# A transformer in one kernel: weight tiles woven column by column in SBUF, and the two TensorE operands placed 128 bytes apart

## The reference, cut to what matters

```
def swiglu(x, w_gate, w_up, w_down):
    return (jax.nn.silu(x @ w_gate) * (x @ w_up)) @ w_down
...
        x = x + 0.5 * rmsnorm(swiglu(h, w1_gate[i], w1_up[i], w1_down[i]), g_ffn1_post[i])
        h = rmsnorm(x, g_mix_pre[i])
        (sb_q, sb_k, sb_v, c_q, c_kv, k_rope_raw, cv_b, cv_c, cv_h) = jnp.split(h @ w_in[i], split_at, axis=-1)
...
        x = x + rmsnorm(mixed @ w_out[i], g_mix_post[i])
```

## Time and profile before

| | before |
|---|---|
| three runs | 3332.34, 3334.76, 3337.73 us; median 3334.76 |
| span of the profiled execution | 3337.3 us |
| matmuls, PE busy | 19480, 3229.6 us (97%) |
| weight loads, PEld busy | 2729.8 us (82%) |
| DVE, ACT, POOL busy | 2059.6, 1359.2, 1345.4 us |
| DMA | 362.59 MB, mean 109 GB/s |

### The profile page before, as it was taken

How to read it: one execution, slowest core, us unless ns; L and a number is a source line. 1 busy time by engine, 2 the same in 40 slices (tenths; PEclk the granted TensorE clock), 3 DMA queues, 4 the chain that set the end, 5 groups by cost and what they waited for, 6 DMA issues and landing times.

```text
span 3337.3 us, 51827 instructions
## 1 busy us (share of the span) xinstructions
PE 3229.6 (97%) x19480; PEld 2729.8 (82%) x19487; DVE 2059.6 (62%) x2673; ACT 1359.2 (41%) x2335; POOL 1345.4 (40%) x643
## 2 busy tenths in 40 slices
PE   8999999999999999999999999998999999999998
PEld 7998775789877899877579987765789987879986
DVE  7774444586647876354477765678477734477753
ACT  5553225344435445322444543324435521254542
POOL 6320562554116541065164404656553107635300
PEclk9999999999999999999999999999999999999999
DMA  4543221255332454322035533221145433215532
GB/s 156 159 143 104 90 87 32 70 152 151 114 123 83 138 160 120 105 83 87 19 99 153 153 117 108 101 68 34 51 135 166 123 103 108 82 57 146 168 104 95
DMA packets 99977, 362.59 MB, mean 109 GB/s; under 512 B 11088, under 2 KB 11344, under 8 KB 99536
## 3 DMA queue, kind: packets, MB, share of 16 engines
q1 hardware_dynamic: 88704, 320.90, 29.4%
q0 software_dynamic: 7776, 28.32, 5.1%
q10 hardware_dynamic: 3312, 10.86, 0.9%
HBM read 355.84 MB, written 4.19 MB: 108 GB/s over the span
## 4 chain that ended last, share of the span: by engine, by line
PE 73%; DVE 10%; issue 6%; ACT 4%; POOL 3%; DMA 3%; DVEq 0%; ACTq 0%; POOLq 0%; SPq 0%
PE psC L749 4%; PE psC L751 4%; PE psC L750 4%; PE psA L749 4%; PE psA L751 4%; PE psA L750 4%; PE psD L899 2%; PE psD L900 2%; PE psD L901 2%; PE psB L899 2%; PE psB L900 2%; PE psB L901 2%; DVE WL L2240 2%; DMA Y<-in_ws 2%; PE psB L984 2%
## 5 line engine op out<-in xcount | busy, mean ns | idle before, releaser
L629 POOL TENSOR_TENSOR WH<-raw,scalars 128x1024 fp32r<-128x1024 f32 (+1 forms) x194 | 377.8, 1948 | 1206.5 <-DMA raw<-in_w 1143.3
L2240 DVE TENSOR_TENSOR WL<-raw,WH 128x1024 fp32r<-128x1024 f32 x324 | 447.9, 1385 | 70.5 <-POOL raw L663 39.8
L631 POOL TENSOR_TENSOR WL<-raw,WH 128x1024 fp32r<-128x1024 f32 (+1 forms) x194 | 471.2, 2429 | 15.2
L1697 ACT ACTIVATE WH<-raw 128x1024 fp32r<-128x1024 f32 x324 | 340.4, 1053 | 48.9 <-DMA raw<-in_ws 37.2
L2316 DVE TENSOR_TENSOR WL<-raw,WH 128x1024 fp32r<-128x1024 f32 (+1 forms) x144 | 163.1, 1135 | 307.4 <-ACT WH L1718 305.8
L658 POOL TENSOR_TENSOR raw<-raw,Y 128x1024 f32<-128x1024 f32 x54 | 133.4, 2471 | 509.6 <-DMA raw<-in_ws 509.6
L1718 ACT ACTIVATE WH<-raw 128x1024 fp32r<-128x1024 f32 (+1 forms) x144 | 141.9, 989 | 375.7 <-DMA raw<-in_w 375.7
L749 PE MATMUL psA<-HH,WH 128*128 128x512 f32 x560 | 230.0, 411 | 0.0
L751 PE MATMUL psA<-HL,WH 128*128 128x512 f32 x560 | 218.5, 390 | 0.0
L750 PE MATMUL psA<-HH,WL 128*128 128x512 f32 x560 | 218.3, 390 | 0.0
L899 PE MATMUL psD<-TH,WH 128*128 128x256 f32 x720 | 202.0, 281 | 6.2 <-DVE psC L2287 2.7
(11 more groups left out here) (540 smaller groups left out, 9631.1 us busy)
## 6 DMA issues: line engine op xcount, KB each, us to landing
raw<-in_w SPq DMA_DIRECT2D x338, 512.0 KB, 3.5
raw<-in_ws SPq DMA_DIRECT2D x216, 512.0 KB, 3.6
Y<-in_ws SPq DMA_DIRECT2D x54, 512.0 KB, 4.7
raw<-in_ws POOLq DMA_DIRECT2D x54, 512.0 KB, 5.4
X<-in_x ACTq DMA_DIRECT2D x4, 512.0 KB, 9.5
NRAW<-in_mem ACTq DMA_DIRECT2D x2, 1024.0 KB, 7.2
out<-Y SPq DMA_DIRECT2D x8, 256.0 KB, 2.1
POSI<-in_pos ACTq DMA_DIRECT2D x4, 256.0 KB, 2.6
```

The source lines that it names most:

```text
L629: pool.tensor_tensor(WH[j][:, 0:w], raw[j][:, 0:w], zero[:, 0:1].broadcast_to([P, w]), ALU.subtract).then_inc(w_hi, 1)
L631: pool.tensor_tensor(WL[j][:, 0:w], raw[j][:, 0:w], WH[j][:, 0:w], ALU.subtract).then_inc(w_split, 1)
L1697: act.activation(WH[slots[i]][:], DX if i == 6 else raw[slots[i]][:], ACT.Copy).then_inc(part_hi, 1)
L2240: dve.tensor_tensor(WL[slots[i]][:], DX if i == 6 else raw[slots[i]][:], WH[slots[i]][:], ALU.subtract).then_inc(part_lo, 1)
```

## The change

The host interleaves each two neighbouring tiles column by column: column c of tile 2j is float 2c of their 256, and column c of tile 2j+1 is float 2c+1. The kernel reads a tile as 128 floats with a step of two (`woven`). Buffers are shifted, so that every weight slot begins at byte 0 modulo 256 and every activation tensor that is a moving operand of the products with pieces begins at byte 128. Some small tensors are laid over others to make room. The pieces of the latent heads, of five tiles at most, are now split six tiles wide, since tile 4 shares its columns with tile 5.

```
-    slot_at = [region(8 * KB) for _ in range(RING)]
+    region(LINE)                     # LINE = 128
+    slot_at = [region(8 * KB) for _ in range(RING)]
...
+    region((LINE - at[0]) % (2 * LINE))
     ar = region(88 * KB)
-    slot_at += [ar + 72 * KB, ar + 80 * KB, ar + 28 * KB, ar + 36 * KB, ar + 64 * KB, SQo, Yo + 8 * KB]
+    slot_at += [ar + 72 * KB - LINE, ar + 80 * KB - LINE, ar + 28 * KB - LINE, ar + 36 * KB - LINE, ar + 64 * KB - LINE, SQo, Yo + 8 * KB]
...
-    sum_at = [ar + 48 * KB, ar + 56 * KB, ar + 72 * KB, ar + 80 * KB]
+    sum_at = [ar + 48 * KB - 2 * LINE, ar + 56 * KB - 2 * LINE, ar + 72 * KB, ar + 80 * KB]
...
+    woven = lambda t: slice(t // 2 * 2 * P + t % 2, (t // 2 + 1) * 2 * P, 2)
...
-            rounds(MH, KQ + KKV)
+            rounds(MH, KQ + KKV + 1)
...
-                w = slice((first_tile + t) * P + cols[0], (first_tile + t) * P + cols[1])
+                w = woven(first_tile + t)
                 pe.matmul(out, WH[slot][:, w], hi[:, t], start=start and t == 0, stop=False)
                 pe.matmul(out, WL[slot][:, w], hi[:, t], start=False, stop=False)
...
-                    w = slice((half * HALF_K + k) * P, (half * HALF_K + k + 1) * P)
+                    w = woven(half * HALF_K + k)
...
+    weave = lambda w: np.ascontiguousarray(w.reshape(-1, P, TILES // 2, 2, P).swapaxes(3, 4)).reshape(-1, P, TILES * P)
+    return weave(out), weave(pairs)
```

More of the change, by code:

```diff
@@ L147, in sb @@
         return nc.alloc_sbuf_tensor_at(name, list(shape), dt, offset=o)
-    KB = 1024
+    KB, LINE = 1024, 128
     X = sb("X", [P, KD, S])
@@ L171, in program @@
     VALL = sb("VALL", [P, DEPTH * NV + NW])
-    VL = sb("VL", [P, NV])
+    VLo = region(320)
+    VL = sb("VL", [P, NV + 4], offset=VLo)
     tabM = sb("tabM", [P, 2, S])
-    scalars = sb("scalars", [P, 4])
+    scalars = VL[:, NV:]
     zero, epsc, lnsc = (scalars[:, i:i + 1] for i in range(3))
-    stat = sb("stat", [P, 8, 4])
-    top8 = sb("top8", [P, QB, 8])
+    stat = sb("stat", [P, 8, 4], offset=RYo + KB)
+    top8 = sb("top8", [P, QB, 8], offset=VLo)
     WIT = sb("WIT", [P, QB, IDXH], offset=RYo)
+    region((LINE - at[0]) % (2 * LINE))
     ar = region(88 * KB)
-    slot_at += [ar + 72 * KB, ar + 80 * KB, ar + 28 * KB, ar + 36 * KB, ar + 64 * KB, SQo, Yo + 8 * KB]
+    slot_at += [ar + 72 * KB - LINE, ar + 80 * KB - LINE, ar + 28 * KB - LINE, ar + 36 * KB - LINE, ar + 64 * KB - LINE, SQo, Yo + 8 * KB]
     raw = [sb(f"raw{j}", [P, TILES * P], offset=o) for j, o in enumerate(slot_at)]
@@ L743, in next_slot, with piece @@
             return (taken - 1) % RING
-        def piece(slot, out, hi, lo, tiles, start=True, stop=True, cols=(0, P), first_tile=0, done=piece_used):
+        def piece(slot, out, hi, lo, tiles, start=True, stop=True, first_tile=0, done=piece_used):
             for t in range(tiles):
-                w = slice((first_tile + t) * P + cols[0], (first_tile + t) * P + cols[1])
+                w = woven(first_tile + t)
                 pe.matmul(out, WH[slot][:, w], hi[:, t], start=start and t == 0, stop=False)
@@ L755, in chunk_high @@
         def chunk_high(slot, out, k, skip=False):
-            w = slice(k * P, (k + 1) * P)
+            w = woven(k)
             pe.matmul(out, WH[slot][:, w], HH[:, k], start=k == 0, stop=False, skip_group_check=skip)
@@ L760, in chunk_low @@
         def chunk_low(slot, out, k, skip=False):
-            mm = pe.matmul(out, WH[slot][:, k * P:(k + 1) * P], HL[:, k], start=False, stop=k == KD - 1, skip_group_check=skip)
+            mm = pe.matmul(out, WH[slot][:, woven(k)], HL[:, k], start=False, stop=k == KD - 1, skip_group_check=skip)
             if k == KD - 1:
@@ L795, in half_chunk @@
         def half_chunk(slot, out, k, half):
-            w, at = slice(k * P, (k + 1) * P), tokens_of(half)
+            w, at = woven(k), tokens_of(half)
             pe.matmul(out[:, at], WH[slot][:, w], HH[:, k, at], start=k == 0 and half == 0, stop=False, skip_group_check=True)
@@ L980, in ffn @@
                     for m in range(EARLY_M):
-                        w = slice((j * EARLY_M + m) * P, (j * EARLY_M + m + 1) * P)
+                        w = woven(j * EARLY_M + m)
                         pe.matmul(down_bank(m), WH[slot][:, w], HIDH[:, k], start=k == 0, stop=False)
@@ L1014, in half_piece @@
                     mean_square_of_first_half()
-                w = slice(t * P, (t + 1) * P)
+                w = woven(t)
                 pe.matmul(out, WH[slot][:, w], hi[:, t, tokens], start=start and i == 0, stop=False)
@@ L1386, in heads_piece @@
                     pe.wait_ge(ol_ready, n.now(ol_ready) - late[t])
-                w = slice((first_tile + t) * P, (first_tile + t + 1) * P)
+                w = woven(first_tile + t)
                 pe.matmul(out, WH[slot][:, w], OH[which][:, t], start=i == 0, stop=False)
@@ L2691, in _ @@
             dve.tensor_scalar(VL[:, 0:16], VALL[:, bass.ds(layer * NV, 16)], 0.5, None, ALU.mult)
-            dve.tensor_scalar(VL[:, 16:], VALL[:, bass.ds(layer * NV + 16, NV - 16)], 1.0, None, ALU.mult).then_inc(vec_ok, 1)
+            dve.tensor_scalar(VL[:, 16:NV], VALL[:, bass.ds(layer * NV + 16, NV - 16)], 1.0, None, ALU.mult).then_inc(vec_ok, 1)
             dve.wait_ge(vec_ok, n.full(vec_ok))
@@ L2931, in weight_stream @@
     assert at == PIECES, (at, PIECES)
-    return out.reshape(PIECES, P, TILES * P), pairs.reshape(FFNS * PAIRS * 4, P, TILES * P)
+    weave = lambda w: np.ascontiguousarray(w.reshape(-1, P, TILES // 2, 2, P).swapaxes(3, 4)).reshape(-1, P, TILES * P)
+    return weave(out), weave(pairs)
 def vectors(a, inv):
```

## The result

| | before | changed |
|---|---|---|
| median of the runs on one chip | 3335.65 us (4 runs) | 3369.8 us (4 runs, 3368.78 to 3373.3) |
| ratio | 1 | 1.0103, 95% interval 1.0089 to 1.0117 |
| span of the profiled execution | 3337.3 us | 3368.8 us |

The forecast was 3230 us with a range of 3175 to 3290. The kernel became 34 us slower in place of 105 us faster.

The account below looks back on a forecast made before the run. TensorE's matmul pace, set by operand placement, was taken to bound the kernel. Gains of 51.0 + 33.6 + 20 = 104.6 us took the span from 3337.3 to 3232, the median to 3230 us; range 3175 to 3290.

Parts of the forecast that it names:

- What bounds the kernel: Whole kernel: TensorE's pace binds (PE busy 97%), 512-column matmuls 13 to 20 ns over their columns depending on operand place.
- the way round through `DX`: FFN pairs: load, two sums, VectorE's queue, load; 19.45 us, a second limit within 0.2 us of TensorE's 19.65.
- How fast without the disturbance?: Matmuls with pieces: 216.5 ns for 512 columns, between 213.3 and 220; 109.5 ns for 256 columns.
- The terms of 51.0 and 33.6 us: 512-column gains: 51.0 us from 3036 `HID` matmuls, 33.6 us from the rest, 48.0 us counted at 0.7.
- Why should it go away?: Load beside stream: with a step of two both addresses move at the same speed, keeping a distance of 128 bytes.
- The argument that the pattern is longer than 128 bytes: 64 ahead and 64 behind differ (229.1, 233.3 ns), so a constant 128 is not the same as 0.
- Cost of the step: Weight loads with a step of two: between nothing and 8 ns, at most 1.3 us a pair; taken as nothing.
- The pairs' term of 20 us gain: FFN pairs: 8.4 us from looped pairs, 7.6 from last pairs, 4 from TensorE's lead; together 20 us.
- all seven products would go alike: Pairs: sign in PE's timeline, all seven products at 110 ns, with TensorE idle before lines 899.
- The sign that I had named: Pairs: the forecast is wrong if the pace of step-two loads is above 117, or pairs fall to 18.4 us.
- Wider splits: 16 pieces go from 640 to 768 floats on GpSimd; some 10 us without cover, counted as nothing.
- the slower one: Rival, 14%: reads 128 bytes apart collide at every column; slower over 230 and 117 ns, worst case over 4900 us.

Follow-up runs that it names:

- pieces_only: Against the changed kernel, pairs put back (parts packed, `TH` and `TL` 64 bytes below weights), 512-column pieces still interleaved: 3342.87 us, ratio 1.0020 to before.

## Why the prediction was wrong

- **What bounds the kernel:** right. TensorE's pace binds, and the operands' place decides the pace. The 19.45 us of the way round through `DX` were a limit for gains. For a loss they were a cover only where that way was the longer one already: pairs 3 to 8 of the second and fourth FFN went from 20.23 and 19.98 us to 20.35, those of the other four from 19.65 to between 20.35 and 20.40.
- **"How fast without the disturbance?" is the step that failed.** I took 216.5 ns from the bf16 row (110 ns for 256 columns) as if it bounded float32r as well. Bf16 does go at 216 and 109 ns, but float32r at 226.7 and 113.3 at the best of 64 distances, with a load of 8 columns no less (231.2 and 113.4). Of the 13 to 20 ns that the forecast wanted to remove, no placement tried removes the first 13.4. What a placement can give is 6.6 ns for `HID`, 2.4 for `HH` in arena slots, and nothing for `HH` in the ring, which already was at the best distance. The terms of 51.0 and 33.6 us had at most 20 and a few us in them.
- **"Why should it go away?"** Wrong too, and this turned the gain into a loss. With equal speed and a constant distance the pace is 231.4 ns, and it hardly depends on the distance (229.9 to 233.6). The packed tile that passes through every distance can be better than that. The argument that the pattern is longer than 128 bytes was right (packed, 0 has 226.7 and 128 has 232.4) but says only that 128 differs from 0, not that it is better; I had no row for 128.
- **"Cost of the step", taken as nothing:** 6 ns a load. I had an upper end of 8 ns and thought it hidden. Under 512 columns it is. Under 256 columns it is not, since 118 ns of load is longer than the 113.3 of a good stream: three of the four `TH` products of a pair could only get worse. That the 8 ns were an upper end was luck. They came from float32 transposes with a step of four, 118 ns, and float32r weights with that same step take 233.5.
- **What the pairs lost:** 0.56 us a pair (20.36 against 19.80) in pairs 3 to 8 and 4.0 ns x 168 in the last ones: 20 + 4 = 24 us by these, 21.7 over all pairs. With the step alone it is 13.7 and with the shifts alone 7.7, so the step is the larger part of it and not the whole.
- **The pairs' term of 20 us gain:** fell with the two above. That all seven products would go alike was right (120.9 to 121.3), and at the wrong value. The sign that I had named, step-two loads above 117 ns in the pairs, came: 118 alone, and 121 in the pairs.
- **Wider splits, counted at nothing:** agrees; GpSimd's busy time rose by 4.8 us, from 1345.4 to 1350.2, and it is in 0% of the chain.
- **The rivals:** the slower one (14%) had its condition met, 231.4 over 230 and 121.1 over 117. Its mechanism, that load and stream shut each other out at every column, didn't happen: nothing near 325 ns. The Trainium skill (TensorE: Matmul & The Clock Gate, What happens when you issue a matmul) has two independent read ports, with which the placing would be worth nothing; the paces from 226.7 to 237.3 ns of the same matmuls speak against that for float32r, while bf16 agrees to 0.1 ns at three distances. Loads of 8 columns keep the excess under 512 columns, which would fit independent ports; loads of 32 columns lose it under 256, which would not. The runs leave the cause open.

Worked out from the mean paces in the two traces: `HID` 3036 x -1.9 and `OH` and `CH` 492 x -1.8 ns, `HH` and the others 3712 x 3.7 (227.6 to 231.3), the 256-column ones of `HID` 264 x 7.5 and of `NH` and `NL` 192 x 3.2, and the pairs' 24: -5.8 - 0.9 + 13.7 + 2.0 + 0.6 + 24 = 33.6 us. Measured were 34. That close an agreement is partly luck, since the same terms without the pairs give 9.6 for `pieces_only`, where 6.3 were measured.

What stays open is why the distance acts on float32r at all, where its first 13.4 ns come from, and why the same operands can have two paces. No run here tells it.

## What to carry to other kernels

Before pricing the removal of an excess, find its floor in the same data type: a small kernel with nothing but the operation, at all placements, costs one run, and it would have turned this forecast round. A load that is hidden under a stream of one width may be exposed under half of it, so a cost that is "hidden" has to be checked at the shortest stream that uses it. And when a layout is changed for all uses at once, look for the uses that are already at their best; here the pay lay in moving only the others (`HID` and the other arena tensors to distance 0: 0.9947, with product 5 moved too 0.9942).

## What the runs showed of the hardware that was not expected

- Float32r matmuls of 128 x 128 by 512 columns go at 226.7 to 237.3 ns by the distance of their operands modulo 256 bytes, bf16 ones at 215.8 at all three distances tried. With 256 columns it is 113.3 to 123.0 and 109.2.
- The best distance depends on the stream: 0 is among the best for 512 columns and 64 for 256, and no distance is among the best for both. At 64 the same 256-column products go at 113.3 or 114.4 ns at one time and at 117.8 at another.
- A weight load of 128 float32r columns takes 111.7 ns packed, 118 at a step of two floats and 233 at a step of four. With a step of four a stream of 256 columns takes 233 to 237 ns.
- VectorE and GpSimd at work in SBUF without a pause change none of 54 paces by more than 0.1 ns, and 512 KB DMAs none of the 27 of 512 columns.
